# Seams between the stages of a hybrid diffusion trunk: stores, first loads and first norms moved across them

## The reference

```python
mod_x = silu(c) @ w_mod + b_mod                   # 3072 columns: shift, scale, gate; the same for c_ctx
sh_x, sc_x, gt_x = split(mod_x, 3)
hx = rmsnorm(x, norm_g) * (1 + sc_x) + sh_x       # hc: the same for the context tokens
px = hx @ w_in                                    # q k v z_a, beta and a gates, hy_v x1 x2, z_b, g_a g_b
ox = deltanet(px, states of the context)          # chunked gated delta rule, both directions, then a norm per head
yx = hyena(px)                                    # two long convolutions by FFT
m = sigmoid(g_a) * (ox @ w_pa) + sigmoid(g_b) * (yx @ w_pb)
out = rmsnorm(x + gt_x * (m @ w_out), final_g)
```

## Time and profile before

| | |
|---|---|
| median of three runs | 4446.98 us |
| the profiled execution | 4446.54 us |
| its span, first to last instruction | 4444.8 us |
| PE busy | 4225.1 us (95%) |
| DVE, ACT, POOL busy | 55%, 28%, 39% |
| front | 0 to 129.4 us |
| projection | 129.4 to 2307.7 us |
| delta | 2307.7 to 2895 us |
| Hyena | 2895 to 3732.6 us |
| merge | 3732.6 to 4444.8 us |

### The profile page before, as it was taken

How to read it: one execution, slowest core, us unless ns; L and a number is a source line. 1 busy time by engine, 2 the same in 40 slices (tenths; PEclk the granted TensorE clock), 3 DMA queues, 4 the chain that set the end, 5 groups by cost and what they waited for, 6 DMA issues and landing times. The chain is left out here.

```text
span 4444.8 us, 72318 instructions
## 1 busy us (share of the span) xinstructions
PE 4225.1 (95%) x28915; PEld 2587.0 (58%) x28915; DVE 2437.7 (55%) x3482; ACT 1233.2 (28%) x2592; POOL 1752.8 (39%) x1487
## 2 busy tenths in 40 slices
PE   5899999999999999999979999989999996999998
PEld 3466544444445544444437888856565654767776
DVE  4555755542446668896616666657676763222221
ACT  4122121111222211111115555555555551000000
POOL 1222233332333343433339989845444451111111
PEclk7999999999999999999989999999999997999999
DMA  6323222223242342425337788567767677223320
GB/s 232 103 74 98 76 94 82 76 95 115 82 154 85 107 117 81 123 76 166 108 128 210 217 261 248 165 178 229 223 195 230 213 246 273 76 76 115 111 76 29
DMA packets 481064, 627.05 MB, mean 141 GB/s; under 512 B 120928, under 2 KB 379944, under 8 KB 470124
## 3 DMA queue, kind: packets, MB, share of 16 engines
q1 hardware_dynamic: 431596, 484.22, 35.9%
q0 software_dynamic: 28560, 113.25, 7.9%
q10 hardware_dynamic: 20592, 25.16, 1.7%
HBM read 405.01 MB, written 217.53 MB: 140 GB/s over the span
## 5 line engine op out<-in xcount | busy, mean ns | idle before, releaser
L1458 PE MATMUL proj_b<-shared_S,proj_tw 128*128 128x512 f32 x1920 | 850.8, 595 | 0.0
L1458 PEld LDWEIGHTS proj_b<-shared_S,proj_tw 128*128 128x128 f32 x1920 | 361.7, 191 | 433.9 <-issue 433.5
L1458 PE MATMUL proj_b<-shared_A,shared_wt 128*128 128x512 f32 x1280 | 577.4, 594 | 13.0 <-PEq L159 12.3
L820 POOL TENSOR_TENSOR proj_tw<-shared_wt 128x512 f32<-128x512 f32 x80 | 109.9, 1374 | 921.3 <-PE proj_b L1458 838.6
L1458 PEld LDWEIGHTS proj_b<-shared_A,shared_wt 128*128 128x128 f32 x1280 | 243.8, 191 | 317.5 <-issue 317.1
L1458 PE MATMUL proj_b<-shared_A,proj_tw 128*128 128x512 f32 x640 | 289.4, 595 | 3.2 <-DVE proj_u L1125 3.2
L1458 PE MATMUL proj_b<-shared_S,shared_wt 128*128 128x512 f32 x640 | 290.9, 597 | 0.0
L1023 ACT ACTIVATE proj_v<-proj_b 128x512 f32<-128x512 f32 x80 | 47.8, 597 | 634.9 <-PE proj_b L1458 634.9
L1840 DVE SCALAR_TENSOR_TENSOR delta_la<-delta_kkq,delta_sc,delta_wm 128x256 f32<-128x256 f32 (+1 forms) x288 | 121.6, 464 | 173.3 <-PE delta_kkq L1939 173.2
L1458 PEld LDWEIGHTS proj_b<-shared_A,proj_tw 128*128 128x128 f32 x640 | 122.2, 191 | 157.6 <-issue 152.6
L1704 POOL TENSOR_SCALAR delta_ex<-delta_rows,delta_sc 128x128 f32<-128x128 f32 x288 | 203.5, 721 | 22.5 <-DMA delta_tnc<-scratch_Tn 22.5
(11 more groups left out here) (333 smaller groups left out, 8583.1 us busy)
## 6 DMA issues: line engine op xcount, KB each, us to landing
shared_wt<-in_w_in_dram POOLq DMA_DIRECT2D x80, 1024.0 KB, 6.0
delta_nv<-scratch_NV SPq DMA_DIRECT2D x144, 256.0 KB, 4.1
delta_kq<-scratch_KQ SPq DMA_DIRECT2D x128, 256.0 KB, 4.3
scratch_bounce_f<-tail_first SPq DMA_DIRECT2D x128, 256.0 KB, 4.4
tail_yf<-scratch_bounce_f SPq DMA_DIRECT2D x32, 1024.0 KB, 7.3
scratch_bounce_i<-fft_yi SPq DMA_DIRECT2D x64, 512.0 KB, 3.4
fft_second<-scratch_bounce_i SPq DMA_DIRECT2D x32, 1024.0 KB, 8.6
scratch_hy<-proj_tok SPq DMA_DIRECT2D x48, 512.0 KB, 2.6
```

Source lines behind the costliest of these rows:

```text
L820: pool.tensor_tensor(T3, w[:, hi, second], w[:, lo, second], ALU.subtract).then_inc(combined, 1)
L1458: last = pe.matmul(bank[:, :], weights[:, k, :], aa[operand][:, k, :], start=(k == 0), stop=(k == KH - 1))
```

## The change

**Front.** The weight pieces are loaded into the not yet used operands S1 to S4 of `aa` instead of `hB`, and the four gate pieces go to four places (`wmg`, parts of `xin`, `xs`) with a semaphore each. All 18 tiles are handled in one run, with one piece after every second tile; `vectors(q)` follows every fourth. Then come the windows. ACT's order is `shape` 0, 1, 2, `keep` 0, 1, `shape` 3, `keep` 2, `shape` 4, `keep` 3, 4. For windows 3 and 4 `split(w)` gives DVE three channel blocks and ACT five. The four sums of each half are made together (`sums(3)`, `sums(5)`). The weights of the first two projection steps are loaded after the eight pieces. At the end SP waits for the gate row and for the stores of A11, A12, A22 (`b_out`) alone; `hA`, from which the sums are stored, is now shared with the projection, whose SP, ACT and DVE wait for those four stores (`comb_out`) before step 1.

```diff
-                for j in range(HEAD_PIECES, NPIECES):
-                    if j > HEAD_PIECES:
-                        sp.wait_ge(products, j)
-                    sp.dma_start(wmg[:, :, :], wv[:, :, j * PIECE_COLS:(j + 1) * PIECE_COLS]).then_inc(wg_in, 16)
+                sp.dma_start(wg[0], gates[:, 0, :, :]).then_inc(wg_in[0], 16)
+                sp.wait_ge(scaled, NCH - 2)
+                sp.dma_start(wg[1], gates[:, 1, :, :]).then_inc(wg_in[1], 16)
...
                 shaped_by_both(sp, 4)
                 for x in ("A11", "A12", "A22"):
-                    sp.dma_start(T["comb"][OPERANDS.index(x)], NEXT[x]).then_inc(S["comb_out"], 16)
+                    sp.dma_start(T["comb"][OPERANDS.index(x)], NEXT[x]).then_inc(S["b_out"], 16)
...
                 sp.wait_ge(row_out, 16)
-                sp.wait_ge(S["comb_out"], 16 * 7)
+                sp.wait_ge(S["b_out"], 16 * 3)
...
-                tiles(0, HEAD_TILES)
+                tiles(0, NCH)
                 for w in range(HEAD):
                     shape(w)
-                for w in range(2):
-                    keep(w)
-                tiles(HEAD_TILES, NCH)
-                for w in range(HEAD, 5):
-                    shape(w)
-                for w in range(2, 5):
-                    keep(w)
+                keep(0)
+                keep(1)
+                shape(3)
+                keep(2)
+                shape(4)
+                keep(3)
+                keep(4)
...
-                for i in range(HEAD_TILES):
+                for i in range(NCH):
                     tile(i)
-                    if i >= 4 and i % 2 == 0:
-                        vectors(i // 2 - 2)
-                    if i >= 2:
-                        piece(i - 2)
+                    if i >= 6 and i % 4 == 2:
+                        vectors(i // 4 - 1)
+                    if i >= 2 and i % 2 == 1:
+                        piece(i // 2 - 1)
                 vectors(3)
+                piece(HEAD_PIECES)
+                for w in range(5):
+                    gate_products(w)
+                    if w < 3:
+                        piece(HEAD_PIECES + 1 + w)
...
+                        gate_turns(w - 1)
```

```diff
+                def pairs_ahead():
+                    last = first_step(1, "k") + H // 2 - 1
+                    sp.wait_ge(inv_out, 64 * NPIECE)
+                    sp.wait_ge(sc_out, 48)
...
+                    sp.dma_start(S["bridge"][:, 0:SC_SIZE], T["sc2"].rearrange("p c h d q -> p (c h d q)")).then_inc(S["sc_in"], 16)
+                    for n in range(AHEAD):
+                        load_pair(sp, T, ring_entry(S["bridge"], SC_SIZE + n * RING_SIZE), n, S["pair_in"][n])
+
                 for s in range(NSTEP + 2):
+                    if s == 1:
+                        sp.wait_ge(S["comb_out"], 16 * 4)
+                    if s == NSTEP - 1:
+                        pairs_ahead()
                     store(s - 2, 1)
...
             @block.gpsimd
             def _(pool):
-                pool.memset(S[:, :, :, :], 0.0).then_inc(cleared, 1)
-                pool.wait_ge(loaded, 48)
+                pool.wait_ge(L["sc_in"], 16)
...
                         differences(n)
+                        if n == 0:
+                            pool.wait_ge(loaded, 32)
                         placements(n)
```

```diff
                 def merge_operands():
                     last = STEPS - 1
-                    ready(pool, "T", last, N2 - 1)
-                    pool.dma_start(tail_w_a(L), T["w_pa"][0].rearrange("(k p) n -> p k n", p=P)).then_inc(L["w_a_in"], 16)
                     ready(pool, "M", last, N2 - 1)
                     for h in range(2):
                         src = T["o"][:, NCTX + h:NCTX + h + 1, :, :, :].rearrange("d a p h t -> p (d a) (h t)")
                         pool.dma_start(tail_o(L)[:, h, :, :], src).then_inc(L["o_in"], 16)
+                    o = tail_o(L)
+                    pool.wait_ge(L["o_in"], 32)
+                    for h in range(2):
+                        pool.tensor_tensor(o[:, h, 0, :], o[:, h, 0, :], o[:, h, 1, :], ALU.add).then_inc(L["summed"], 1)
+                    ready(pool, "O", last, 1)
+                    pool.dma_start(tail_w_a(L), T["w_pa"][0].rearrange("(k p) n -> p k n", p=P)).then_inc(L["w_a_in"], 16)
...
-                sp.dma_start(T["yT"][2 * NCB - 2:2 * NCB, :, :].rearrange("h p t -> p h t"), yt).then_inc(y_stored, 16)
-                sp.wait_ge(y_stored, 16 * NCB)
+                sp.dma_start(T["yT"][2 * NCB - 2:2 * NCB, :, :].rearrange("h p t -> p h t"), yt).then_inc(L["y_out"], 16)
...
+                        if off == 0:
+                            sp.wait_ge(L["y_out"], 16)
```

More of the change, by code:

```diff
@@ L242, in modulate, with split @@
                 "S1": quarter(1, 0), "S2": quarter(1, 1), "S3": quarter(2, 0), "S4": quarter(2, 1)}
+        def split(w):
+            return KH if w < HEAD else KH - 1
         def shaped_by_both(eng, w):
@@ L328, in shape @@
                         act.wait_ge(moved[n], (first + width) // P)
-                    for k in range(KH, KT):
+                    for k in range(split(w), KT):
                         last = act.activation(part(w, k), raw(k, first, width), ACT.Identity, scale=gsc[:, k, a:a + 1], bias=mod[:, k, a:a + 1])
@@ L440, in _ @@
+                tiles(0, NCH, keep_vectors)
                 vectors()
@@ L563, with pair_of, parts_of, ring_entry @@
 PIECE_STEPS = 8
-PRODUCTS = ("P1", "P6", "P7", "P5", "P2", "P4", "P3")
+RING_PART = {"kq": 8 * P, "nv": 8 * P, "rows": 4 * P, "ttc": 4 * SB, "tnc": 4 * SB}
+RING_SIZE = sum(RING_PART.values())
+SC_SIZE = NCH * H * 2 * NQ
+AHEAD = 2
+LOADS = 10
+PRODUCTS = ("P1", "P6", "P7", "P5", "P2", "P4", "P3")
+def pair_of(n):
+    s, j = divmod(n, PAIRS)
+    back = NCTX - 1 - s if s < NCTX else NCH - 1 - (s - NCTX)
+    return (s, back), j
+def parts_of(n):
+    return 2 if n >= FIRST_LATENT else 1
+def ring_entry(flat, base):
+    views, at = {}, base
+    for name, size in RING_PART.items():
+        x = flat[:, at:at + size]
+        if name in ("kq", "nv"):
+            views[name] = x.rearrange("p (d g a t) -> p d g a t", d=2, g=2, a=2)
+        else:
+            views[name] = x.rearrange("p (d g t) -> p d g t", d=2, g=2)
+        at += size
+    return views
+def load_pair(sp, T, ring, n, landed):
+    chunks, j = pair_of(n)
+    for d in range(2):
+        c, heads = chunks[d], slice(2 * j, 2 * j + 2)
+        parts = slice(0, parts_of(n))
+        sp.dma_start(ring["rows"][:, d, :, :].rearrange("p g t -> p (g t)"), T["gcT"][d, c, heads, :].rearrange("h t -> (h t)").unsqueeze(0).broadcast_to([P, 2 * CH])).then_inc(landed, 16)
+        sp.dma_start(ring["kq"][:, d, :, parts, :], T["KQ"][c, :, heads, parts, :]).then_inc(landed, 16)
+        sp.dma_start(ring["nv"][:, d, :, :, :], T["NV"][c, :, heads, :, :]).then_inc(landed, 16)
+        for name, dst in (("Tt", ring["ttc"]), ("Tn", ring["tnc"])):
+            sp.dma_start(dst[:, d, :, :], T[name][d, c, heads, :, :, :].rearrange("h q j i -> (q j) h i")).then_inc(landed, 16)
 def first_step(h, name):
@@ L1623, in delta @@
         S = kit.sb("S", P, H, 2, P)
-        kq, nv = kit.sb("kq", P, DEPTH, 2, 2, 2, P), kit.sb("nv", P, DEPTH, 2, 2, 2, P)
-        rows = kit.sb("rows", P, DEPTH, 2, 2, P)
-        ttc, tnc = kit.sb("ttc", P, DEPTH, 2, 2, SB), kit.sb("tnc", P, DEPTH, 2, 2, SB)
+        later = kit.sb("ring", P, (DEPTH - AHEAD) * RING_SIZE)
+        ring = [ring_entry(L["bridge"], SC_SIZE + i * RING_SIZE) if i < AHEAD else ring_entry(later, (i - AHEAD) * RING_SIZE) for i in range(DEPTH)]
+        kq, nv, rows, ttc, tnc = ([entry[x] for entry in ring] for x in ("kq", "nv", "rows", "ttc", "tnc"))
         tt, tn = kit.sb("tt", P, KEPT, 2, 2, P), kit.sb("tn", P, KEPT, 2, 2, 2 * SB)
@@ L1641, in delta @@
         loaded, cleared = kit.sem("loaded"), kit.sem("cleared")
-        landed = [kit.sem(f"landed{i}") for i in range(DEPTH)]
+        landed = [L["pair_in"][i] if i < AHEAD else kit.sem(f"landed{i}") for i in range(DEPTH)]
         stored = [kit.sem(f"stored{i}") for i in range(2)]
@@ L1938, in k_kq @@
                             out = b_kkq[g][mine, 2 * P * d:2 * P * (d + 1)].rearrange("p (a t) -> p a t", a=2)[:, parts, kept]
[L1939 removed]
+                            last = pe.matmul(out, kq[n % DEPTH][:, d, g, 0, mine], kq[n % DEPTH][:, d, g, parts, kept], start=True, stop=True)
                     last.then_inc(kkq_done, 1)
@@ L2647, in tail_o, with tail_norm @@
     return L["yf"][:, :, :, :].rearrange("p b g c -> p (b g c)").rearrange("p (h d n) -> p h d n", h=2, d=2)
+def tail_norm(L):
+    flat = L["bridge"][:, 28 * CB:]
+    epsq = flat[:, 0:NCH * H].rearrange("p (c h) -> p c h", c=NCH)
+    ms, sd = (flat[:, (NCH + 2 * i) * H:(NCH + 2 * i + 2) * H].rearrange("p (a h) -> p a h", a=2) for i in range(2))
+    return epsq, ms, sd, flat[:, (NCH + 4) * H:(NCH + 4) * H + 1]
 def tail_mix(L):
@@ L2808, in _ @@
                 dve.sem_inc(normed, 2)
```

(8 more changed lines are left out.)

244 lines of the change are left out of this document (134 added, 110 removed).

## The result

The changed kernel takes **4400.41 us** (median of four runs, 4397.23 to 4402.66) against 4447.57 for the kernel before in the same comparison: ratio 0.9897, 95% interval 0.9884 to 0.9909, so 47 us faster. The profiled execution took 4402.66 us (span 4400.6), 2.25 above the median. The forecast was 4395 with a range of 4384 to 4408.

What follows compares the result with a forecast made beforehand. PE is busy 95% of the span, so only its idle times at stage seams can be won: 4446.5 - 20.5 (front) - 9.9 (delta) - 21.1 (Hyena to merge) = 4395 us, own range 4387 to 4404, eight in ten 4384 to 4408.

Steps and rivals of the forecast that it cites:

- Front: First stage, all tiles first, then shaping: next stage at 108.9 instead of 129.46, 20.5 us gained (14 to 28).
- The pace of 2.8 us a tile: Front's tile loads: 2.8 us each, between bounds of 3.05 (nothing gained) and 2.4; square 17 starts at 55.4.
- The shaping chain: Front, after the tiles: window shaping and gate products take 21.8 us, 2.3 of the chain for product 2; done at 86.5.
- The tail: Front's end, everything shaped to next stage: 23.3 us, less 0.9 because fewer stores are waited for.
- Rival A: Front: the tile ring is quick, 2.4 us a tile; 5.2 us more gained, 4390; chance 0.13.
- Delta: Projection to delta: loading ahead starts GpSimd's first difference at once, 10.55 us less 0.6 for masks; 9.9 us gained.
- more than 2178 us: Sign of being wrong: this long between projection's first matmul and the delta block means the loads ahead cost it.
- Rival D: Delta: operands' new places lengthen GpSimd's work; gain used up at 0.72 us per pair, 4467 at 1 us; chance 0.03.
- Hyena's drain: Hyena's end: with `w_pa` behind it, the last operand's read goes 10.5 us earlier (7 to 12.7); PE's wait near 12.
- Merge's start: Merge's beginning: block start 6.3 us earlier without the store's wait, first turn 6.5 more, first weighing another 1.0.
- Merge's first window and behind it: Merge: SP's loads move only 12.5 us, so PE waits 3.2 us for the first gated bank, four products in.
- rival C: Merge's first window hangs on SP's loads alone, 4404 (8.6 more); or the front's ring stays at 3.05, 4398; chance 0.20.

Runs made afterwards that it cites:

- run 3: Changed kernel, but the first gate piece (1 MB) is issued only when 16 tiles are scaled: 4401.3 us.
- runs 1 and 2: Changed kernel with the gate row stored by ScalarE's queue, 4391.83 us; changed kernel with SP waiting for all seven stores at the front's end, 4401.61 us.
- Run 5: Changed kernel, but delta's scalars and first two pairs are loaded at that stage's start, not in the last projection step: 4409.99 us.
- run 7: Changed kernel, but only one of eight heads of the first window's `o` is loaded (0.25 MB instead of 2 MB; output not the reference's): 4392.94 us.
- run 6: Changed kernel, but `w_pa` (4 MB) is again loaded before `o` at Hyena's end: 4407.75 us.
- run 8: Changed kernel, but `w_out` (4 MB) is issued from ScalarE's queue once the second window's `o` has landed, not ahead of it on SP's: 4399.93 us.

## Why the prediction was right, and where it was off

The time came out 5.4 us over the forecast, and no step failed in its mechanism. The profiled execution is 7.3 us short of the forecast's gain of 51.5 (44.2), and these are the terms. Runs price the tail, the loads ahead, the order of the two loads, the place of `w_out` and the wait for the store; no run puts back the old order of tiles and windows, which makes most of the front's gain, or the norms' old place, so these are read from the landmarks of the two profiles alone.

**Front, 19.2 for 20.5.** The pace of 2.8 us a tile was right for tiles 4 to 14 (2.80), under the traffic that I had in mind. What the sum had wrong is that it holds to the end: tile 15 came 6.46 us after tile 14 (5.6 to 6.9 in the ten other profiles with software loads), in a time when the software queue moved hardly a packet (run 3), so square 17 was 2.2 us late. From there to shaping it took 10.8 instead of 9.3, so shaping was 3.7 late: PE had stood still for 4.37 us waiting for tile 14's scaling, which stands behind tile 15's mean, and worked the tiles off at a lower clock (granted 0.67 from 55 to 60 us, 0.65 from 60 to 65, against 1.00 from 50 to 55), a tile's eight transposes in 1.95 us instead of 1.09. The shaping chain gave 2.2 back: 19.6 instead of 21.8. That is the 2.3 that the sum has for product 2: it ran beside the shaping of window 3 and nobody waited for it. Two errors of the front so cancel in part, which is luck. The tail was sized right (22.2 for 22.4), and its reason, one row behind seven stores, was shown by runs 1 and 2. Rival A is out: up to tile 14 the tiles came at 2.7 to 3.0 us in all profiles of the changed kernel and its variants, not at 2.4, from either kind of queue.

The stretch with the missing tile and the one behind it (length, busy PE, PEld, DVE, ACT, POOL, granted clock, DMA share, GB/s), and PE's transposes of tile 14:

```profile
50.00:55.00 5.00, 1.46 (x21) 0.64 (x19) 0.26 (x2) 1.45 (x4) 0.14 (x1) 1.00 1.07 385
55.00:60.00 5.00, 4.17 (x22) 3.83 (x23) 4.44 (x10) 3.13 (x8) 0.00 (x0) 0.67 0.57 190
...
55.83 1.21 PE L507 MATMUL mod_b<-mod_ident,bridge_region 128*128 128x128 f32 x8 [4.37 <-DVE bridge_region L389]
```

**Delta, 10.4 for 9.9, of which 2.0 are not there at the stage's end.** Run 5 prices the loads ahead at 9.6 to 10.7 and shows no cost to the projection. (As a sign of being wrong, "more than 2178 us" had no room: the stretch is 2178.2 before the change as well.) The 2.0 I don't take for an effect: the stage took 578.3 us before and 580.3 after, and between 577.1 and 583.3 over the profiles of kernels that leave its work alone. What varies there was not settled. Rival D, slower GpSimd work, is out: its 288 differences are busy for 203.5 us before and 203.6 after.

**Hyena's drain, about 8 for 10.5.** PE's wait fell from 22.14 to 14.19, not to 12. The mis-sized term is the cost of `o`'s 2 MB, which I let go by at the rate of the queue; run 7 measures 4.85 us for 1.75 MB of them. The order of the two loads is worth 8.8 (run 6). The norms cost nothing on VectorE: its last one ended before PE had filled the first output bank.

**Merge's start, 13.4 for 13.8.** The first turn comes 12.4 us sooner after the store's issue (12.8 forecast for block start and turn together), and from it to the first product it is 1.0 less, as worked out.

**Merge's first window and behind it, 5.1 lost for 3.2.** From the first product to `w_out`'s first it takes 64.5 us instead of 59.9, 4.6 of the 5.1; the rest lies behind. The place was right: `o` of the second window behind SP's 8 MB, then norms, then gates, then PE four products on, with a stall of 2.67 us. What I left out is the clock behind the stall. Product 4 took 5.41 us where it took 3.62 before, 1.8 us, more than half of the stall again. The windows of the changed kernel (length, busy PE, PEld, DVE, ACT, POOL, granted clock, DMA share, GB/s), product 4 and the stretch behind it:

```profile
3731.50:3737.00 5.50, 5.42 (x17) 4.51 (x18) 3.13 (x6) 0.00 (x0) 2.80 (x4) 0.69 0.88 314
3737.00:3747.00 10.00, 10.00 (x48) 8.79 (x48) 0.69 (x1) 0.00 (x0) 0.73 (x1) 1.00 0.01 2
```

The granted clock averages 0.69 over the first, a mix of the half level (1.2 GHz) and the full one (2.4), and 1.00 in the second; PE had stood still for 2.67 us ahead of it. In run 8 stall and slow product are both gone. Not every execution pays it: with a stall of 1.3 to 1.75 us (runs 1 to 3) product 4 took 3.72 us, and the window lost 1.7 to 2.6 us, so the forecast's 3.2 lies inside what executions show. This is rival C in part: a first window that hangs on SP's loads, at 5.1 us instead of the 11.8 that it had there (3.2 and 8.6 more).

## What to carry to other kernels

When a wait is taken off a list, look at what remains on it: a small transfer issued last on the same ring stands for all that lie ahead of it, and moving it to another queue can be worth five times the wait. Work that starts earlier finds its next operand behind the same queue as before, so for every seam ask which transfer now ends last, and put large loads that are needed late behind small ones that are needed early. A PE stall can cost the work behind it clock as well (2.67 us did, 1.3 to 1.75 us hardly); take it from a row beside another stall. And a mean pace hides single waits: list each arrival before blaming all of them.

## What the runs showed of the hardware

- Two loads beside a stream of stores that PE waits for cost it time at once: 14.2 us with 2 MB on the software queue, 9.3 with 0.25 MB, 23.0 with 6 MB.
- A 512 KB load took 6.8 us from the software queue and 6.5 from a hardware queue, in the same 30 us of the same program.
- A 4 KB store alone on its ring, issued while the engines were full, had its first packet moved over 3 us after its issue.
- After a stall of 2.67 us, one product of 16 matmuls ran 5.41 us, near the 5.61 of the stage's first one; the next ran at 3.62 again. In six profiles with a stall of 2.66 to 2.71 us the product took 5.41, in three with 1.30 to 1.75 us 3.72.
- Beside a weight piece and 1024 rows of 128 bytes on SP's queue, the software queue moved 36 packets in 4 us where SP's moved 1478, with a tile's load outstanding (46 to 50 us of the changed kernel).
